# Folding the head norms' weights into rotation tables and PSUM copies, and moving one adaptation slab, in a one-core fp32 network kernel

## The reference, cut to what matters

```python
def adaln(cond, w, b):
    return jnp.split(jax.nn.silu(cond) @ w + b, 3, axis=-1)      # shift, scale, gate
# layer ab
h = rms_norm_2(x, norm_g) * (1 + scale) + shift
hc = rms_norm_2(xc, norm_g) * (1 + cscale) + cshift
q = axial_rope(rms_norm_2(q, qn_g)); k = axial_rope(rms_norm_2(k, kn_g))   # heads of 64
ck = rms_norm_2(ck, kn_g);  cq = rms_norm_2(cq, qn_g)                      # context: no rotation
y_a = conformer_conv(...)            # gated conv, then silu(layer_norm(u, ln_g, ln_b))
y = jnp.concatenate([y_a, y_b], axis=-1) * jax.nn.silu(z)
x = x + gate * (y @ w_out);  xc = xc + cgate * (yc @ w_out)
# layer cd: h and hc as above with its own shift and scale, then Fourier mix and attention,
x = x + gate * (y @ w_out)
```

## Time and profile before

| | us |
|---|---|
| median of 3 runs | 1129.09 (1127.7 to 1129.18) |
| profiled execution | 1128.63 |
| its span, first to last instruction | 1126.8 |
| PE busy | 1090.4 (97%) |
| DVE busy | 751.0 (67%) |
| ACT busy | 549.0 (49%) |
| mean granted TensorE clock | 0.993 |

### The profile page before, as it was taken

How to read it: one execution, slowest core, us unless ns; L and a number is a source line. 1 busy time by engine, 2 the same in 40 slices (tenths; PEclk the granted TensorE clock), 3 DMA queues, 4 the chain that set the end, 5 groups by cost and what they waited for, 6 DMA issues and landing times. The chain is left out here.

```text
span 1126.8 us, 17866 instructions
## 1 busy us (share of the span) xinstructions
PE 1090.4 (97%) x7000; PEld 943.2 (84%) x7000; DVE 751.0 (67%) x1456; ACT 549.0 (49%) x985; POOL 43.6 (4%) x55
## 2 busy tenths in 40 slices
PE   8999999999999999999999999999999999999996
PEld 7877879899887877879999988798867888989865
DVE  5774766555555665776887888789765745834475
ACT  5642845444444443855444454535445733623273
POOL 1000001000000000000000000100300000000000
PEclk9999999999999999999999999999999999999998
DMA  9667055555565567047666546843356022864000
GB/s 339 244 217 297 6 164 169 190 190 189 178 203 168 186 203 288 2 150 176 186 206 202 187 159 206 276 150 113 113 192 210 2 88 65 209 159 142 28 18 39
DMA packets 55046, 183.34 MB, mean 163 GB/s; under 512 B 20788, under 2 KB 33460, under 8 KB 35508
## 3 DMA queue, kind: packets, MB, share of 16 engines
q1 hardware_dynamic: 54964, 182.22, 49.5%
HBM read 179.31 MB, written 2.90 MB: 162 GB/s over the span
## 5 line engine op out<-in xcount | busy, mean ns | idle before, releaser
L236 DVE TENSOR_TENSOR w_lo<-ring,w_hi 128x1024 fp32r<-128x1024 f32 x260 | 317.1, 1223 | 203.5 <-ACT w_hi L230 198.7
L230 ACT CAST w_hi<-ring 128x1024 fp32r<-128x1024 f32 x260 | 271.5, 1052 | 323.5 <-PE banks L292 319.5
L292 PE MATMUL banks<-shared_hi,w_hi 128*128 128x256 f32 (+1 forms) x448 | 134.2, 299 | 1.5 <-DVE w_lo L236 1.5
L292 PE MATMUL banks<-shared_lo,w_hi 128*128 128x256 f32 (+1 forms) x448 | 133.7, 298 | 0.0
L292 PE MATMUL banks<-shared_hi,w_lo 128*128 128x256 f32 (+1 forms) x448 | 133.6, 298 | 0.0
L292 PE MATMUL banks<-w_hi,u_hi 128*128 128x512 f32 x256 | 100.0, 390 | 0.0
L292 PE MATMUL banks<-w_lo,u_hi 128*128 128x512 f32 x256 | 99.8, 390 | 0.0
L292 PE MATMUL banks<-w_hi,u_lo 128*128 128x512 f32 x256 | 99.7, 390 | 0.0
L292 PEld LDWEIGHTS banks<-shared_hi,w_hi 128*128 128x128 f32 x448 | 85.7, 191 | 4.2 <-issue 1.7
L292 PEld LDWEIGHTS banks<-shared_hi,w_lo 128*128 128x128 f32 x448 | 85.7, 191 | 2.6
L292 PEld LDWEIGHTS banks<-shared_lo,w_hi 128*128 128x128 f32 x448 | 85.7, 191 | 2.4
(11 more groups left out here) (404 smaller groups left out, 2246.4 us busy)
## 6 DMA issues: line engine op xcount, KB each, us to landing
ring<-in_w_up SPq DMA_DIRECT2D x32, 1024.0 KB, 5.1
ring<-in_w_down SPq DMA_DIRECT2D x32, 1024.0 KB, 5.1
ring<-in_w_in SPq DMA_DIRECT2D x23, 1024.0 KB, 5.2
ring<-in_ab_ada SPq DMA_DIRECT2D x12, 1024.0 KB, 5.2
ring<-in_cd_ada SPq DMA_DIRECT2D x12, 1024.0 KB, 5.0
ring<-in_cd_in SPq DMA_DIRECT2D x12, 1024.0 KB, 7.5
ring<-in_w_out SPq DMA_DIRECT2D x8, 1024.0 KB, 6.6
ring<-in_ab_in SPq DMA_DIRECT2D x16, 512.0 KB, 5.1
```

The costliest lines, as they stand in the source:

```text
L230: nc.scalar.copy(w_hi[:, n % PARTS, :], part_source(key, q)).then_inc(hi_ready, 1)
L236: nc.vector.tensor_tensor(w_lo[:, n % PARTS, :], part_source(key, q), w_hi[:, n % PARTS, :].bitcast(F32), ALU.subtract).then_inc(part_read ...
L292: mm = nc.tensor.matmul(dst, a, b, start=first_one and i == 0, stop=last_one and i == 2, skip_group_check=shares_bank)
```

## The change

The slabs: `cd_heads` takes two slabs (the scales) rather than three, `cd_turn` takes slab 4, and a new place `cd_late` takes slab 5 at the end of the output stage. The head norms' weights: POOL multiplies them into eight small rotation tables (`gained`) in the convolution stage, DVE rotates with these, and the context heads get them as the scale of the copies out of PSUM. The variance: the matmuls move to the heads stage and accumulate two blocks, so that DVE's second addition is left out. The gates of cd are turned and biased in the features stage, in place of its fillers, and written to HBM at the end of SP's list.

```diff
-          "cd_first": (1, 0, 2), "cd_heads": (1, 2, 3), "cd_turn": (1, 5, 1)}
+          "cd_first": (1, 0, 2), "cd_heads": (1, 2, 2), "cd_turn": (1, 4, 1), "cd_late": (1, 5, 1)}
-SECOND_SLABS = [..., ("cd_heads", 3), ("cd_turn", 1), ("ab_out", 2), ("cd_in", 6), ("cd_out", 2)]
+SECOND_SLABS = [..., ("cd_heads", 2), ("cd_turn", 1), ("ab_out", 2), ("cd_late", 1), ("cd_in", 6), ("cd_out", 2)]
# norm_programs, on_tensor
-                if shifts is not None:
+                if behind is not None:
+                    behind()
+                elif shifts is not None:
                     keep_busy(0, 8)
# transpose_groups, tensor
-                        mm = nc.tensor.matmul(banks[:, VARIANCE, 4 * t:4 * t + 4], squares[:, t * P:(t + 1) * P],
-                                              minus_half[:, 0:4], start=True, stop=True)
...
-                    pe.wait_ge(kept, 1)
-                    turn_conditions(rows, row_here).then_inc(row_turned, 1)
-                    keep_busy(burst_bank, 3)
+                    keep_busy(VARIANCE, 5)
# project_features
+                def turn_gates():
+                    turn_conditions(turn_row, banks[:, GATE, 0:16])
+                    turn_conditions(late_row, banks[:, GATE, 16:32]).then_inc(gate_turned, 1)
# its sync
-                    sp.dma_start(gates.rearrange("(c p) -> p c", p=P), ada[:, 1, 16:24, 0],
-                                 allow_slow_non_contiguous=True).then_inc(gates_here, 16)
...
+                    sp.wait_ge(gate_biased, 1)
+                    sp.dma_start(gates.rearrange("(c p) -> p c", p=P), ada[:, 1, 16:24, 0],
+                                 allow_slow_non_contiguous=True).then_inc(gates_here, 16)
                     sp.wait_ge(gates_here, 16)
# its vector
+                    dve.wait_ge(half_used, first[key])
+                    split_lo(dve, key, 1)
+                    for t in (2, 3):
+                        nc.vector.tensor_tensor(x[:, t, right], mixed[:, t, right], x[:, t, right],
+                                                ALU.add).then_inc(ctx_added, 1)
                     norm["vector"](dve)
...
+                        if q == 2:
+                            dve.wait_ge(gate_turned, 1)
+                            add_biases(1, ADA_AT["cd_turn"][1], banks[:, GATE, 0:32], 2).then_inc(gate_biased, 1)
# out_project, tensor / scalar / vector
-                        keep_busy(0, 12)
+                        pe.wait_ge(half_used, first["cd_late"])
+                        adapt_products(pe, "cd_late", 0, 0)
+                        keep_busy(1, 6)
...
+                        keep_adapted(act, "cd_late", 0, 0, late_row)
                         act.wait_ge(own_rstd, 1)
                         nc.scalar.activation(mixed[:, 0, :], x[:, 0, :], ACT.Copy, scale=own_root[:, 0:1])
...
-                    split_ahead(split_lo, dve, key)
+                    if attended is not None:
+                        split_lo(dve, next_key[key], 0)
...
+                        if t >= TT:
+                            nc.vector.tensor_tensor(mixed[:, t, cols], src, gates[t // 2][:, cols], ALU.mult)
+                            continue
# project_and_convolve: sync, gpsimd, vector
+                    for h in range(2):
+                        sp.dma_start(gain_cols[h * HD:(h + 1) * HD, 0:2], ...)
+                    pool.wait_ge(tables_here, 96)
+                    for kind in range(2):
...
+                            nc.gpsimd.tensor_tensor(gained[:, kind, i, :, :], axial[:, table, :, :], gain, ALU.mult)
-                                            mixed[:, 2:4, BANK:2 * BANK], ALU.add).then_inc(added, 1)
-                    dve.wait_ge(added, 1)
-                    nc.vector.tensor_tensor(mixed[:, 0, BANK:2 * BANK], mixed[:, 0, BANK:2 * BANK],
-                                            mixed[:, 1, BANK:2 * BANK], ALU.add)
+                                            mixed[:, 2:4, BANK:2 * BANK], ALU.add)
# prepare_axial_heads: tensor, then vector
+                    for t in range(4):
+                        tok = slice(BANK + t * P, BANK + (t + 1) * P)
+                        accumulate(banks[:, VARIANCE, 4 * t:4 * t + 4],
+                                   [(mixed[:, c, tok], minus_half[:, 0:4]) for c in range(2)])
                     for j in range(SLABS):
                         adapt_products(pe, "cd_heads", j, j)
                     for j in range(SLABS):
                         pe.wait_ge(kept, j + 1)
                         turn_conditions(cd_rows[:, j, :], banks[:, TURNED, 16 * j:16 * (j + 1)]).then_inc(turned, 1)
-                    keep_busy(7, 12)
...
-                    step(apply_gains(own))
-                    rope(dve, step, qk[:, own, :, :], axial[:, 0, :, :], axial[:, 1, :, :], HD // 2, temps)
-                    dve.wait_ge(rows_scaled, 2)
-                    apply_gains(slice(TT, 4))
+                    for i, (dst, src) in enumerate(((c1, x1), (s2, x2), (c2, x2), (s1, x1))):
+                        for kind, heads in ((0, slice(0, B_HEADS)), (1, slice(B_HEADS, H))):
...
+                            last = nc.vector.tensor_tensor(dst[:, :, heads, :], src[:, :, heads, :], table, ALU.mult)
+                    step(last)
+                    nc.vector.tensor_tensor(x1, c1, s2, ALU.subtract)
+                    nc.vector.tensor_tensor(x2, c2, s1, ALU.add)
```

More of the change, by code:

```diff
@@ L565, in products_done @@
             engine.wait_ge(part_used, first_part[key] + 4 * (s + 1))
[L567 removed]
+        VARIANCE = 6
+        rstd_rows, turn_row = ada_rows[:, 2 * D:2 * D + BANK], ada_rows[:, 2 * D + BANK:3 * D]
+        late_row = rstd_rows
         def transpose_groups(groups, burst, behind=None):
             key, burst_bank, rows = burst
[L574 removed]
             here = rstd[:, 48:52]
[L576 to L581, removed]
+            SPREAD = 7
+            with stage("turned", "copied0", "copied1", "variance_ready", "rstd_ready", "spread_ready") as (
+                    turned, copied0, copied1, variance_ready, rstd_ready, spread_ready), nc.Block() as block:
                 @block.sync
@@ L641, in _ @@
                             last.then_inc(copied1, 1)
-                    keep_adapted(act, key, 0, burst_bank, rows).then_inc(kept, 1)
+                    keep_adapted(act, key, 0, burst_bank, rows)
                     act.wait_ge(spread_ready, 1)
@@ L1066, in _ @@
                             advance(lows, 3)
-                    split_ahead(split_lo, dve, key)
+                    if attended is not None:
+                        split_lo(dve, next_key[key], 0)
+                    else:
+                        split_ahead(split_lo, dve, key)
                     advance(lows)
@@ L2991, in prepare_axial_heads @@
             temps = [flat[:, i * 640:(i + 1) * 640] for i in range(4)]
-            SLABS, TURNED = 3, 3
-            with stage("dve_step", "rows_scaled", "kept", "turned") as (
-                    dve_step, rows_scaled, kept, turned), nc.Block() as block:
+            SLABS, TURNED = 2, 3
+            with stage("dve_step", "kept", "turned") as (dve_step, kept, turned), nc.Block() as block:
                 @block.sync
@@ L3005, in _ @@
                         turn_conditions(cd_rows[:, j, :], banks[:, TURNED, 16 * j:16 * (j + 1)]).then_inc(turned, 1)
-                    keep_busy(7, 12)
-                def apply_gains(tiles):
-                    T = tiles.stop - tiles.start
-                    for h0, h1, gain in ((0, B_HEADS, gains[:, 0:HD]), (B_HEADS, H, gains[:, HD:2 * HD])):
-                        here = qk[:, tiles, h0:h1, :]
-                        last = nc.vector.tensor_tensor(
-                            here, here, gain.unsqueeze(1).unsqueeze(1).broadcast_to([P, T, h1 - h0, HD]), ALU.mult)
-                    return last
                 @block.scalar
@@ L3019, in _ @@
                         for h in range(H):
-                            last = nc.scalar.activation(qk[:, t, h, :], qk[:, t, h, :], ACT.Copy,
-                                                        scale=rstd[:, t * H + h:t * H + h + 1])
-                        last.then_inc(rows_scaled, 1)
+                            nc.scalar.activation(qk[:, t, h, :], qk[:, t, h, :], ACT.Copy,
+                                                 scale=rstd[:, t * H + h:t * H + h + 1])
                     for j in range(SLABS):
```

62 lines of the change are left out of this document (39 added, 23 removed).

## The result

The changed kernel took 1121.78 us (median of four, 1120.13 to 1123.51) against 1128.76: ratio 0.9943, interval 0.9931 to 0.9955. Two later sets of it, against the kernel before on the same chip, gave 0.9956 [0.9944, 0.9969] and 0.9951 [0.9934, 0.9967]. So by these ratios it is 0.44 to 0.57% faster, 5.0 to 6.4 us. The medians of the three sets lie 7.0, 3.9 and 4.9 us under those of the kernel before beside them, so the 7.0 of the first set is the high end. The profiled execution took 1123.51, with a span of 1121.7 against 1126.8.

What follows compares the result with a forecast made beforehand. PE, busy 1090.4 of 1126.8 us, was taken as the bound. Terms -0.6 - 8.6 - 1.4 + 0.3 + 0.7 = -9.6 us, plus 1.3 for the clock, gave -8.3: median 1120.8 us, range 1118.0 to 1125.2.

Steps and rivals of the forecast that it cites:

- part 2: Heads stage: PE's new chain takes 7.8 us against 16.36, so -8.6 us, bounds -7.8 to -9.0.
- no fall: Rival: the clock does not fall in the lulls the change leaves; 1119.5 us, chance 0.17.
- Part 1: Convolution stage's end: DVE's second addition goes and PE's fillers end last, -0.6 us; added POOL products and loads cost nothing.
- Part 7: Clock: one stretch at 1.2 GHz, at the heads' end or features' start, +1.3 us, bounds 0 to +3.4.
- Part 3: Turning stage: variance and the turning behind the spread go, two fillers come, -1.4 us, bounds -1.0 to -1.6.
- Part 4: Output stage's end: DVE ends earlier, but ACT is last, waiting for PE's slab products; +0.3 us, bounds -0.3 to +0.8.
- Part 5: Features stage's start: DVE's split and two additions delay the first product, +0.7 us, bounds +0.3 to +1.2.
- Part 6: DMA ring and cd's gates: later requests and gate write cost 0, with five us of cover in the features stage.
- rival A: Clock falls at both heads' end and features' start, or for the long stretch: +3.4 us, 1122.9 us, chance 0.20.
- C: Another engine holds the heads' end or features' start, DVE's products costing 1.1 a pair: 1123.1 us, chance 0.12.
- D: Slower than before: clock falls at the heads' end and stays at 1.2 GHz in attention; 1132 us, chance 0.04.
- E: Removed filler covered something else, e.g. SP's ring requests at the heads' end: at most 1 us, chance counted in C.

Runs made afterwards that it cites:

- the kernel whose clock stayed up there: Changed kernel with its eight variance matmuls placed between the two slabs of the heads stage: 1122.00 us, ratio 0.9946 to the kernel before.
- fillers: Kernel before with only the 12 filler matmuls (24 records) at the heads stage's end removed: 1127.79 us, ratio 0.9994.
- fold: Kernel before with only the head norms' weights folded into tables and copy scales, three slabs and filler matmuls kept: 1128.75 us, ratio 1.0009.
- slab's move: Changed kernel with gains on DVE, 24 filler records back at the heads' end, eight variance matmuls in the turning stage: 1128.97 us, ratio 1.0001 to the kernel before.
- variance moved away: Changed kernel with the eight variance matmuls moved from the heads stage to the turning stage's start, DVE waiting: 1126.76 us, ratio 0.9985 to the kernel before.

## Why the prediction was right, and where it was not

The forecast was 1120.8 with a range of 1118.0 to 1125.2; the first set gave 1121.78. The low end of the range was worked out wrong: part 2 at -9.0 and no fall make 1129.09 - 10.0 = 1119.1, not 1118.3; the measured time does not lie between the two. Point by point:

- **Part 1, convolution end.** -0.6 forecast, 111.54 to 110.94 measured. GpSimd's eight added products (4.43 us in all) and two loads stayed hidden.
- **Part 2, heads.** The chain at full clock was sized well: 7.8 forecast, 8.05 in the kernel whose clock stayed up there. DVE's products took 3.30 for the 3.32 assumed, and PE, not DVE, ended the stage. But the stage took 9.58, outside my bounds, since part 7's stretch fell into it.
- **Part 3, turning.** -1.4 forecast, -1.34 measured; the terms listed give -1.6 (1.03 + 0.95 + 0.1 - 0.5), so the sum was taken smaller than its terms, and that came out. **Part 4**: +0.3 and +0.40, with ACT last, for the reason given. **Part 5**: +0.7 and +0.89. **Part 6**: 0 as forecast; the read was issued 12.3 us behind the write, for about 11, and landed 4.8 us later, for 8, so the cover was 1057.95 - 1050.6 = 7.4 us, for five.
- **Part 7, the clock, is the step that was wrong in its place and short in its number.** I put one fall at the heads' end or the features' start, as I counted only waits and the turning products as thin work. It comes 2 to 3 us behind the heads' *start*, behind the stage's gap and the eight variance matmuls, 16 records of four columns (1.92 us), and the slabs behind them pay (5.34 for 3.64, +1.7 for the 1.3 forecast; 9.58 for 8.05 in the stage, +1.5). All seven profiles of kernels that start this stage with the variance show it; the four edits of the changed kernel that start it with a slab have every slab record of the stage at full speed. I had moved this variance ahead of the slabs in the sum without asking what it does to the clock. That a stretch of 3.4 us and not 6.8 would follow held in two of the changed kernel's three profiles (the third has 3.4 + 3.4 + 3.5 us in the touched stages), and its price was right within 0.4.
- **Forecast or rival A?** The sum as forecast was -8.3 us; the touched stages gave -7.0 in the first profile, 0.5 of the difference in heads and 0.4 behind the features stage. Of the 15 executions of the changed kernel in three sets, six took 1120.10 to 1121.69 us at mean clocks of 0.994 to 0.996, and nine 1123.18 to 1125.53 at 0.992 to 0.993. The first group lies at the forecast, the second at or above A's 1122.9, and the median of all 15 is 1123.2; the first set, two and two, lay between by luck.
- **A's time is not A's mechanism.** All three profiles are of the second group. Only the third (1125.53) has falls at more than one place in the touched stages; the first and second (1123.51, 1123.81) have one there, and another at about 13 us, in code that nobody touched and where the profile of the kernel before has none. So two of three reached A's time for a reason that the prediction had nowhere, and no execution of the first group was profiled. A at 0.20 was still too low: the features' start had a low stretch in 6 of the 11 profiles of kernels with the late slab (one of the changed kernel's three), and in none of the three without.
- **Rivals C, D and E** did not happen: PE ends the heads stage, attention ran at 1.00 at 49.15 us, and the fillers covered nothing but the clock.

What I would not have got from the rows is how little the parts are worth alone: fillers 0.9994, fold 1.0009, slab's move 1.0001; together 0.995. Two things were shown. Some parts hold each other up: DVE's 9.4 us of gains stand behind PE's 16 (fold alone: nothing), and ACT's scaling of 4.9 us stands behind the slabs (variance moved away: 1.7 of 3.6). And a part taken out of thin surroundings lengthens the low stretch: 10.2 or 10.3 us for 6.9 in two of the three kernels that have one part alone (mean clocks of 0.9922 and 0.9925 over their 11 and 12 executions, for 0.9943). What of it brings the clock down, the waits, the stage's end or the matmuls of four columns, stays open: none was changed alone. Nor was the variance's move tried alone on the kernel before.

## What to carry over

Where TensorE is the bound, list for each stretch what it does between dense products: stage gaps, waits and matmuls of a few columns. Where they follow one another, try breaking the row with dense work that has to be done anyway before trying fillers: here it took the fall out of the stage at no cost of its own, though alone its gain in the whole kernel could not be told. Test parts of a change together as well as alone: here three parts of which none gave anything measurable gave 0.5% together. And judge a difference of 0.2% by executions at like clock, not by one trace: two profiles of one kernel had their low stretches at different places.

## What the runs showed of the hardware

- **Time goes with the mean granted clock.** Over 159 executions, each against the mean of its own kernel's set, 0.001 of mean clock is 0.90 us (I had expected 1.1). The low stretches in these stages add up to about 3.4 us or two or three times that, and cost at most half their length.
- **A fall can come or not in the same kernel.** The changed kernel has a low stretch at about 13 us in two profiles and none at the features' start, and in the third none at 13 us but one in turning and one at the features' start. The Trainium skill (TensorE: Matmul & The Clock Gate, Part 1: The HAM clock gate) says that the gate looks in a rhythm of its own and that the same kernel varies from run to run; the profiles agree that it varies.
- **GpSimd's additions held DVE up**: a pair of its operations took 1.63 us for 0.75, though their data had nothing in common. What it cost GpSimd was not measured.
- **A write of 4-byte elements to HBM** (4 KB) took 12.3 us until what waited for it could start. In the kernel before it stood at the head of the features stage, and the queues moved 27 GB/s over the 11 us behind it; with it gone from there they moved 361 GB/s (949 to 960). The stage got no shorter by that: 109.0 us before, 109.9 after.
